# Last four experts: gate and up loaded as whole matrices, the final weights' spread moved behind the transposes, and part of the way back moved ahead of the last product

## The chip, the cores and the metric

The kernel runs on one core of one Trainium2 chip. The metric is the device time of one execution in microseconds, lower is better. The executions of the kernel before took 438.43 to 440.27 us, with a median of 439.71 us.

## What is computed

One decoder layer on 256 tokens of width 1024, in fp32. Two attention mixers and a cross-attention come first. Then comes a mixture of experts: 32 experts in 4 groups, every token goes to its best group and there to its two best experts. A final RMS norm with a gain closes the layer. The part that matters here:

```
hid = (silu(einsum('nd,edf->nef', hf, w_gate[g]))
       * einsum('nd,edf->nef', hf, w_up[g]) * combine[:, g, :, None])
out = out + einsum('nef,efd->nd', hid, w_down[g])
...
x = x + hier_moe(rmsnorm(x, ffn_norm_g[l]), ...)
return rmsnorm(x, final_norm_g)
```

Each expert has a gate and an up matrix of 1024 x 256 and a down matrix of 256 x 1024, all of them 1 MB. The weights of all 32 experts, 96 MB, are read once from the chip's main memory; this stream lasts through the second half of the kernel.

## The kernel before

**Quads and slots.** The experts are worked through four at a time, a "quad". For one quad 32 tokens per expert are gathered, so that the four experts fill the 128 columns of the array side by side, each in a tile of 32. A quad's weights are 12 chunks of 1 MB (MOE_CHUNKS): chunks 0 to 7 are gate and up, chunks 8 to 11 are down. They land in 24 slots of 8 KB per partition; two neighbouring slots make one tensor `moe_pair`. SyncE (SP) issues all loads in one fixed order. It waits for `chunk_used` before each, a count that TensorE raises when it has read a chunk. All weights travel in one queue, first in first out, and some 20 to 28 us of them are queued ahead of what is being moved.

**One quad on TensorE** goes like this: gather(0) for the first half of k, the 1024-long contraction being cut into 8 steps of 128 (gather, L1760, writes the banks `score0` and `score1`; VectorE multiplies by gains and copies to `moe_x`, L1317); the gate and up products of k 0 to 3; gather(1) into the same banks and the same `moe_x`; the gate and up products of k 4 to 7. ScalarE makes silu of the gate product (L887) and VectorE multiplies by the up product (L1335, `hid`). TensorE transposes the selection matrix (L1844) and then `hid` (L1848), and ScalarE copies the latter out (L889, `hidT`). Then follow the down products and the "way back": a product with the weighted selection `selwT` that adds the experts' results to the tokens' sums in the banks ACC (`attno0`, `attno1` for the first 512 columns of tokens 0 to 127 and 128 to 255, `proj1`, `probt1` for the second 512).

**Formats of the loads.** Quad 0's first use is loaded in small runs. Quads in the middle are "whole" (`load_whole`): one DMA for each matrix of one expert, with 8 KB in a row on each partition. The last quad (experts 28 to 31, `load_last`, L456 to L469) is loaded for an early start of its products: gate and up as (half of k, gate or up, pair of experts), two DMAs of 512 KB for each chunk, with 4 KB runs (`load_gate_or_up`, L436); down as columns of all four experts, 2 KB runs, and the last chunk in two parts with 1 KB runs (L468).

**The last quad** (`last_quad`) differs in three ways from the others. Its gate and up products go by (half of k, gate or up) as the chunks come (`gate_up_by_columns`, L1814): gate k 0 to 3, up k 0 to 3, gather(1), gate k 4 to 7, up k 4 to 7. Ahead of that last piece it spreads the row of final gains to all 128 partitions by two products with a row of ones (L1803, into `score0` and `score1`); VectorE copies them to `fin_g` (L1332). And its second 512 columns come in two pieces of 256 (`down_last_columns`, L1894), which VectorE copies to `y1_last` (L1348), and then the way back in four products (`back_last_columns`, L1900). ScalarE squares the finished sums for the final norm (L655); means, root and scaling follow (L921, L594, L1373, L1375, L911), and the output goes out in four DMAs.

An fp32 product appears in the trace as two MATMUL records: a row "x32" is 16 products.

## Time and profile before

| | us |
|---|---|
| median of the timed executions | 439.71 |
| lowest and highest of them | 438.43, 440.27 |
| the profiled execution, whole | 438.02 |
| its span (first to last instruction) | 436.3 |
| TensorE busy | 395.9 (91%) |
| VectorE / ScalarE / GpSimd busy | 190.4 / 155.0 / 36.0 |

The span is what the trace shows; the 1.7 us between it and 438.02 lie around it. Of the 436.3 us about the last 30 belong to the last quad. The shares of busy time are averages over unlike stages, so they say little about a change in the last 30 us; for that one reads the chain of waits and the order in time in this stretch.

### The profile page before, as it was taken

What the parts mean: (1) busy time and instruction counts of PE and PEld (TensorE: products, weight loads), DVE (VectorE), ACT (ScalarE), POOL (GpSimd) and SP (SyncE); (2) the same over time, 40 slices, a digit from 0 to 9 for tenths busy, and PEclk for the clock granted to TensorE, in tenths of its full rate; (3) what the DMA queues carried; (4) which work ended last, traced back from release to release, by engine and by line L of the source; (5) the groups of instructions that cost most, each with busy time, mean ns of one, the idle gap of its engine ahead of it and who ended that gap; (6) DMA issues with size and microseconds to landing.
All of it is one profiled execution on the core that took longest, in us unless ns stands there. A gap on an engine that the chain in (4) does not pass through costs nothing.

```text
span 436.3 us, 7016 instructions
## 1 busy us (share of the span) xinstructions
PE 395.9 (91%) x2761; PEld 278.0 (64%) x2761; DVE 190.4 (44%) x358; ACT 155.0 (36%) x299; POOL 36.0 (8%) x80
## 2 busy tenths in 40 slices
PE   7999999999999999999999989899878838758984
PEld 7998897777788888999796634434333303313632
DVE  3675667866667846754655211221212102102123
ACT  6633565576358444485737110100000000001013
POOL 4010122224000000010401200000000000000001
PEclk9999999999999999999999999999999959969999
DMA  7978776767777668897758899999999999999993
GB/s 243 302 223 281 231 263 215 235 206 241 258 241 268 202 232 292 276 332 225 270 218 361 331 424 421 415 420 421 422 422 423 421 421 422 421 421 409 409 380 120
DMA packets 48770, 138.95 MB, mean 318 GB/s; under 512 B 5191, under 2 KB 19559, under 8 KB 39528
## 3 DMA queue, kind: packets, MB, share of 16 engines
q1 hardware_dynamic: 48528, 138.31, 85.0%
q8 instruction: 17, 0.28, 0.3%
q10 hardware_dynamic: 216, 0.28, 0.2%
q14 instruction: 9, 0.07, 0.0%
HBM read 137.54 MB, written 1.05 MB: 318 GB/s over the span
## 4 chain that ended last, share of the span: by engine, by line
PE 75%; DMA 12%; SPq 5%; DVE 3%; ACT 1%; issue 1%; POOL 1%; DVEq 0%; POOLq 0%; ACTq 0%
DMA moe_pair<-in_expert_w_up_dram 12%; PE proj L1407 10%; PE proj L1408 9%; PE proj L1409 9%; PE proj L1833 7%; SPq L428 5%; PE score L1760 4%; PE score L1856 4%; PE attno L1408 2%; PE attno L1409 2%; PE attno L1407 2%; PE attno L1905 2%; PE proj L1787 2%; PE attno L1551 1%; PE probt L1409 1%; PE probt L1408 1%
## 5 line engine op out<-in xcount | busy, mean ns | idle before, releaser
L945 DVE TENSOR_TENSOR w_lo<-w_raw,w_hi 128x1024 fp32r<-128x1024 f32 x64 | 78.3, 1226 | 37.1 <-ACT w_hi L682 36.8
L682 ACT ACTIVATE w_hi<-w_raw 128x1024 fp32r<-128x1024 f32 x64 | 67.9, 1060 | 40.4 <-DMA w_raw<-in_w_in_dram 11.1
L1833 PE MATMUL proj<-moe_pair,moe_x 128*32 128x512 f32 x384 | 47.4, 637 | 19.6 <-DMA moe_pair<-in_expert_w_up_dram 19.6
L1317 DVE TENSOR_TENSOR moe_x<-score,gains_moe 128x256 f32<-128x256 f32 x32 | 13.6, 425 | 93.3 <-PE score L1760 93.1
L887 ACT ACTIVATE hid<-proj 128x256 f32<-128x256 f32 x8 | 3.1, 383 | 136.8 <-PE proj L1833 112.8
L1833 PEld LDWEIGHTS proj<-moe_pair,moe_x 128*32 128x32 f32 x384 | 11.8, 116 | 45.9 <-issue 44.8
L1760 PEld LDWEIGHTS score<-sel,xg 128*128 128x128 f32 x256 | 30.5, 192 | 10.6 <-issue 10.0
L1407 PE MATMUL proj<-hT_hi,w_hi 128*128 128x256 f32 x112 | 32.3, 288 | 0.8 <-DVE w_lo L1024 0.8
L1760 PE MATMUL score<-sel,xg 128*128 128x128 f32 x256 | 32.5, 279 | 0.0
L1409 PE MATMUL proj<-hT_hi,w_lo 128*128 128x256 f32 x112 | 31.7, 283 | 0.0
L1408 PE MATMUL proj<-hT_lo,w_hi 128*128 128x256 f32 x112 | 31.7, 283 | 0.0
L1856 PE MATMUL score<-moe_pair,hidT 128*32 128x512 f32 x240 | 27.4, 595 | 3.8 <-ACT hidT L889 3.8
L594 POOL TENSOR_TENSOR rnorm<-mean_eps,mhalf 128x1 f32<-128x1 f32 x10 | 5.8, 586 | 299.2 <-DVE mean_eps L921 299.2
L1407 PE MATMUL proj<-w_hi,hT_hi 128*128 128x512 f32 x64 | 25.9, 404 | 0.0
L1408 PE MATMUL proj<-w_lo,hT_hi 128*128 128x512 f32 x64 | 25.0, 391 | 0.0
L1409 PE MATMUL proj<-w_hi,hT_lo 128*128 128x512 f32 x64 | 25.0, 391 | 0.0
L610 POOL TENSOR_SCALAR scores<-scores,rinv 128x128 f32<-128x128 f32 (+1 forms) x32 | 18.1, 584 | 64.7 <-DVE rinv L983 64.7
L1407 PEld LDWEIGHTS proj<-hT_hi,w_hi 128*128 128x128 f32 x112 | 21.4, 191 | 2.2 <-DVE w_lo L1024 1.0
L1408 PEld LDWEIGHTS proj<-hT_lo,w_hi 128*128 128x128 f32 x112 | 21.4, 191 | 0.0
L1409 PEld LDWEIGHTS proj<-hT_hi,w_lo 128*128 128x128 f32 x112 | 21.4, 191 | 0.0
L708 ACT ACTIVATE scores<-scores,nmax 128x128 f32<-128x128 f32 (+1 forms) x32 | 14.2, 445 | 14.7 <-DVE sink_arg L970 7.7
L1856 PEld LDWEIGHTS score<-moe_pair,hidT 128*32 128x32 f32 x240 | 7.0, 109 | 18.5 <-issue 12.8
(345 smaller groups left out, 731.9 us busy)
## 6 DMA issues: line engine op xcount, KB each, us to landing
moe_pair<-in_expert_w_gate_dram SPq DMA_DIRECT2D x28, 1024.0 KB, 13.2
moe_pair<-in_expert_w_up_dram SPq DMA_DIRECT2D x28, 1024.0 KB, 15.0
moe_pair<-in_expert_w_down_dram SPq DMA_DIRECT2D x27, 1024.0 KB, 24.9
w_raw<-in_w_in_dram SPq DMA_DIRECT2D x33, 512.0 KB, 4.4
moe_pair<-in_expert_w_down_dram SPq DMA_DIRECT2D x10, 512.0 KB, 6.5
w_raw<-in_xattn_wkv_dram SPq DMA_DIRECT2D x8, 512.0 KB, 4.4
w_raw<-in_mix_out_w_dram SPq DMA_DIRECT2D x8, 512.0 KB, 5.0
moe_pair<-in_expert_w_gate_dram SPq DMA_DIRECT2D x8, 512.0 KB, 20.1
```

The costliest lines, as they stand in the source:

```text
L428: sp.dma_start(slots[s][:].unsqueeze(1), src).then_inc(moe_in[s], 16)
L610: pool.tensor_scalar(scores[:, j % 2, hh, cols], scores[:, j % 2, hh, cols], rinv[:, j % 2, i:i + 1], 1.0, ALU.mult, ALU.mult).then_inc(s_ ...
L682: act.activation(w_hi[g % NS][:], w_raw[:, g % NW], ACT.Copy).then_inc(hi_done, 1)
L708: act.activation(scores[:, b, hh, cols], scores[:, b, hh, cols], ACT.Exp, bias=nmax[:, b, tt, hh:hh + 1], accum_out=rsum[:, b, i:i + 1]).t ...
L945: dve.tensor_tensor(w_lo[g % NS][:], w_raw[:, g % NW], w_hi[g % NS][:].bitcast(F32), ALU.subtract)\
L1317: dve.tensor_tensor(moe_x[:, pair], SC[u % 2][:, 0:2 * P].rearrange("p (k s) -> p k s", k=2), gains_moe[:, u // 2, pair].unsqueeze(2) .bro ...
L1407: pe.matmul(ps, a[0], b[0], start=start, stop=False, skip_group_check=True)
L1408: pe.matmul(ps, a[0], b[1], start=False, stop=False, skip_group_check=True)
L1409: return pe.matmul(ps, a[1], b[0], start=False, stop=stop, skip_group_check=True)
L1760: op = pe.matmul(SC[u % 2][:, (k % 2) * P:(k % 2 + 1) * P], xg[:, t, k * P:(k + 1) * P], sel[:, t].rearrange("p e s -> p (e s)"), start=t ...
L1833: op = pe.matmul(PJ[0][e * WIN:(e + 1) * WIN, :].rearrange("p (j f) -> p j f", j=2), moe_x[:, k % 4, e * WIN:(e + 1) * WIN], pair[:].rearr ...
L1856: return pe.matmul(SC[half][e * WIN:(e + 1) * WIN, :], hidT[:, kt, e * WIN:(e + 1) * WIN], weights, start=kt == 0, stop=kt == KF - 1)
```

## The change

1. Gate and up of the last quad are loaded as whole matrices of one expert, 8 DMAs of 1 MB with 8 KB runs in place of 16 of 512 KB with 4 KB runs: first the four gates, then the four ups. The down loads stay as they were.
2. TensorE does all of gate (k 0 to 3, gather(1), k 4 to 7), then all of up; it waits for all four gates ahead of the one and for all four ups ahead of the other. As up k 0 to 3 now comes after the second gather, the gathered tokens of the second half get a buffer of their own, `moe_x_late`. ScalarE's silu waits for the gate alone.
3. The spread of the final gains is cut in two: its first product stands between the transposes of `hid` and the first down product (bank `proj0`), its second between the two steps of the first down product (bank `score1`). VectorE copies both after `hid` and `selwT`.
4. The way back of the last 512 columns is no longer one block at the end: the first product for tokens 0 to 127 stands before the last down product, the one for tokens 128 to 255 right after it. The semaphore is raised by each product, and the squares wait for two.

```diff
             def load_last(c):
                 s, e0 = slot_of_chunk(LAST_QUAD * MOE_CHUNKS + c), NE - QE
                 if c < GU_CHUNKS:
-                    load_gate_or_up(c, s, e0, ends_in[c])
+                    j, e = divmod(c, QE)
+                    sp.dma_start(slots[s][:].unsqueeze(1), whole_v[j][:, e0 + e:e0 + e + 1, :])\
+                        .then_inc(ends_in[c], 16)
...
-            expert_quad(more * 2 + 3, GU_CHUNKS - 2)
+            expert_quad(more * 2 + 3, QE)
...
-                    act.wait_ge(back_ps[t][half], more * 2 + 4)
+                    act.wait_ge(back_ps[t][half], more * 2 + 4 + half)
...
-                    dve.tensor_tensor(moe_x[:, pair],
+                    gathered = moe_x_late if next_experts is None and u >= 2 else moe_x
+                    dve.tensor_tensor(gathered[:, pair],
...
-                if next_experts is None:
-                    for h in range(2):
-                        dve.wait_ge(fin_g_ps, h + 1)
-                        dve.tensor_copy(fin_g[:, h * 512:(h + 1) * 512], SC[h][:]).then_inc(fin_g_set, 1)
                 dve.wait_ge(silu_done, n + 1)
...
                 if next_experts is None:
+                    for h, bank in enumerate((PJ[0], SC[1])):
+                        dve.wait_ge(fin_g_ps, h + 1)
+                        dve.tensor_copy(fin_g[:, h * 512:(h + 1) * 512], bank[:]).then_inc(fin_g_set, 1)
                     dve.wait_ge(fin_g_set, 2)
...
+            def gate_then_up(n):
+
+                for j in range(2):
+                    for e in range(QE):
+                        pe.wait_ge(ends_in[j * QE + e], LAST_WHOLE_LANDED)
+                    for k in range(KD):
+                        if j == 0:
+                            if k == KD // 2:
+                                gather(1)
                             if k % 2 == 0:
                                 pe.wait_ge(moe_x_sb, n * 4 + k // 2 + 1)
+                        gathered = (moe_x, moe_x_late)[k // 4]
+                        for e in range(QE):
+                            w = slots[slot_of_chunk(LAST_QUAD * MOE_CHUNKS + j * QE + e)][:]
+                            op = pe.matmul((PJ[0][:, 0:FE], LAST_UP)[j][e * WIN:(e + 1) * WIN],
...
             def back_last_columns(t, i):
 
-                return pe.matmul(ACC[t][1][:, i * CW:(i + 1) * CW], selwT[:, t * P:(t + 1) * P],
-                                 y1_last[:, i * CW:(i + 1) * CW], start=False, stop=True, skip_group_check=True)
+                pe.wait_ge(y1_sb_set, i + 1)
+                pe.matmul(ACC[t][1][:, i * CW:(i + 1) * CW], selwT[:, t * P:(t + 1) * P],
+                          y1_last[:, i * CW:(i + 1) * CW], start=False, stop=True, skip_group_check=True)\
+                    .then_inc(back_ps[t][1], 1)
...
             def last_quad(n):
 
-                gate_up_by_columns(LAST_QUAD, n, ends_in, LAST_UP)
+                gate_then_up(n)
+                transposes(n, hid_halves)
+                pe.wait_ge(fin_in, 16)
+                pe.wait_ge(ones_row_set, 1)
+                spread_gains(PJ[0], 0)
+                pe.wait_ge(hidT_sb, n + 1)
+                down_first_columns(0)
+                pe.wait_ge(selT_sb, n + 1)
+                spread_gains(SC[1], 1)
+                down_first_columns(1).then_inc(y0_ps, 1)
                 pe.wait_ge(fin_g_set, 2)
-                transposes(n, hid_halves)
-                pe.wait_ge(hidT_sb, n + 1)
-                down_first_columns().then_inc(y0_ps, 1)
-                pe.wait_ge(selT_sb, n + 1)
                 pe.wait_ge(y_act, n + 1)
                 back_to_tokens(0, 0)
                 back_to_tokens(1, 0)
...
                 down_last_columns(0, 1).then_inc(y1_ps, 1)
+                back_last_columns(0, 0)
                 pe.wait_ge(last_cols_in, 16)
                 down_last_columns(1, 1).then_inc(y1_ps, 1)
+                back_last_columns(1, 0)
                 for t in range(TT):
-                    for i in range(2):
-                        pe.wait_ge(y1_sb_set, i + 1)
-                        op = back_last_columns(t, i)
-                    op.then_inc(back_ps[t][1], 1)
+                    back_last_columns(t, 1)
```

The order on TensorE, first around the up product of the last quad and the spread. `proj0` holds the gate product, `probt0` the up product; names that begin with `first_and_last_loaded` are the landings of the last quad's chunks. Before:

```order
L1814 MATMUL proj0<-moe_pair8_93,moe_x_107 32x256 [waits moe_x_sb]
L1814 MATMUL proj0<-moe_pair8_93,moe_x_107 32x256 x7
L1803 MATMUL score0<-g_row_125,ones_row_126 128x512 [waits ones_row_set,fin_in]
L1803 MATMUL score1<-g_row_125,ones_row_126 128x512
L1814 MATMUL probt0<-moe_pair9_94,moe_x_107 32x256 [waits moe_x_sb,first_and_last_loaded7,first_and_last_loaded6]
L1814 MATMUL probt0<-moe_pair9_94,moe_x_107 32x256 x7
L1814 MATMUL probt0<-moe_pair9_94,moe_x_107 32x256 [waits moe_x_sb]
L1814 MATMUL probt0<-moe_pair9_94,moe_x_107 32x256 x7
```

The same place after the change:

```order
L1799 MATMUL proj0<-moe_pair6_91,moe_x_late_126 32x256 x2
L1799 MATMUL proj0<-moe_pair7_92,moe_x_late_126 32x256 x2
L1799 MATMUL probt0<-moe_pair8_93,moe_x_107 32x256 [waits first_and_last_loaded6,first_and_last_loaded7,first_and_last_loaded5,first_and_last_loaded4]
L1799 MATMUL probt0<-moe_pair8_93,moe_x_107 32x256
L1799 MATMUL probt0<-moe_pair9_94,moe_x_107 32x256 x2
L1799 MATMUL probt0<-moe_pair8_93,moe_x_107 32x256 x2
```

The spread is gone from here, and the wait for the last two chunks, which stood ahead of 16 products of up, now stands with that for two more ahead of all 32.

From the transposes of `hid` to the first way back, before:

```order
L1848 MATMUL probt0<-ident_152,hid_110 128x128 [waits hid_done]
L1848 MATMUL probt0<-ident_152,hid_110 128x128
L1856 MATMUL score0<-moe_pair10_95,hidT_111 32x512 [waits first_and_last_loaded8,hidT_sb]
L1856 MATMUL score0<-moe_pair10_95,hidT_111 32x512 x3
L1856 MATMUL score0<-moe_pair10_95,hidT_111 32x512 [waits first_and_last_loaded9]
L1856 MATMUL score0<-moe_pair10_95,hidT_111 32x512 x3
L1905 MATMUL attno0<-y0_sb_108,selwT_112 128x512 [waits y_act,selT_sb]
```

and after:

```order
L1833 MATMUL probt0<-ident_153,hid_110 128x128 [waits hid_done]
L1833 MATMUL probt0<-ident_153,hid_110 128x128
L1875 MATMUL proj0<-g_row_125,ones_row_127 128x512 [waits ones_row_set,fin_in]
L1841 MATMUL score0<-moe_pair10_95,hidT_111 32x512 [waits first_and_last_loaded8,hidT_sb]
L1841 MATMUL score0<-moe_pair10_95,hidT_111 32x512 x3
L1875 MATMUL score1<-g_row_125,ones_row_127 128x512 [waits selT_sb]
L1841 MATMUL score0<-moe_pair10_95,hidT_111 32x512 [waits first_and_last_loaded9]
L1841 MATMUL score0<-moe_pair10_95,hidT_111 32x512 x3
L1896 MATMUL attno0<-y0_sb_108,selwT_112 128x512 [waits y_act,fin_g_set]
```

One spread product now stands ahead of each step of the first down product.

The end of TensorE's program, before:

```order
L1894 MATMUL score1<-moe_pair11_96,hidT_111 32x256 [waits first_and_last_loaded11]
L1894 MATMUL score1<-moe_pair11_96,hidT_111 32x256 x3
L1894 MATMUL probt0<-moe_pair11_96,hidT_111 32x256 [waits last_columns_loaded]
L1894 MATMUL probt0<-moe_pair11_96,hidT_111 32x256 x3
L1900 MATMUL proj1<-y1_last_124,selwT_112 128x256 [waits y1_sb_set] x2
L1900 MATMUL probt1<-y1_last_124,selwT_112 128x256 [waits y1_sb_set] x2
```

and after:

```order
L1883 MATMUL score1<-moe_pair11_96,hidT_111 32x256 [waits first_and_last_loaded11]
L1883 MATMUL score1<-moe_pair11_96,hidT_111 32x256 x3
L1890 MATMUL proj1<-y1_last_124,selwT_112 128x256 [waits y1_sb_set]
L1883 MATMUL probt0<-moe_pair11_96,hidT_111 32x256 [waits last_columns_loaded]
L1883 MATMUL probt0<-moe_pair11_96,hidT_111 32x256 x3
L1890 MATMUL probt1<-y1_last_124,selwT_112 128x256 [waits y1_sb_set]
L1890 MATMUL proj1<-y1_last_124,selwT_112 128x256 [waits y1_sb_set]
L1890 MATMUL probt1<-y1_last_124,selwT_112 128x256 [waits y1_sb_set]
```

The last down product now stands behind a wait for VectorE's copy of the one before it.

## Rows read from the trace of the kernel before

**Rows 1.** The page: the span, and the span in 40 slices of 10.9 us.

```profile
span 436.3 us, 7016 instructions
...
DMA  7978776767777668897758899999999999999993
```

**Rows 2.** DMA view: packets and rate from 381 to 393 us, whole matrices.

```profile
DMA packets 695, 5.05 MB, mean 421 GB/s; under 512 B 78, under 2 KB 78, under 8 KB 78
```

**Rows 3.** DMA view: the same from 397 to 413 us, last quad's gate and up.

```profile
DMA packets 1798, 6.55 MB, mean 410 GB/s; under 512 B 198, under 2 KB 198, under 8 KB 1798
```

**Rows 4.** One load each: issue (start us, us) and us to landing. Chunk 7, chunk 9, last columns.

```profile
400.70 0.43 SPq L436 DMA_DIRECT2D moe_pair<-in_expert_w_up_dram  x1
moe_pair<-in_expert_w_up_dram SPq DMA_DIRECT2D x1, 512.0 KB, 15.9
...
404.27 4.38 SPq L468 DMA_DIRECT2D moe_pair<-in_expert_w_down_dram  x1
moe_pair<-in_expert_w_down_dram SPq DMA_DIRECT2D x1, 1024.0 KB, 17.8
...
415.88 2.54 SPq L468 DMA_DIRECT2D moe_pair<-in_expert_w_down_dram  x1
moe_pair<-in_expert_w_down_dram SPq DMA_DIRECT2D x1, 512.0 KB, 11.6
```

**Rows 5.** The chain that ended last, in time: start us, us, what.

```profile
408.95 1.86 PE proj L1814 x32
...
412.54 1.98 PE score L1760 x16
414.53 1.86 PE proj L1814 x32
416.39 1.91 PE score L1803 x4
418.30 1.94 PE probt L1814 x32
...
420.73 0.45 PE probt L1848 x2
...
421.64 1.97 PE score L1856 x16
...
424.38 1.95 PE attno L1905 x4
...
427.33 0.48 PE score L1894 x8
...
427.83 0.44 DVE y_last L1348
...
428.31 1.14 PE proj L1900 x4
429.45 0.88 PE probt L1900 x4
```

**Rows 6.** Timeline, ScalarE's squares at the end and TensorE's down product for the last columns.

```profile
427.58 0.63 PE L1894 MATMUL probt<-moe_pair,hidT 128*32 128x256 f32 x8
...
429.49 0.60 ACT L655 ACTIVATE fin_rows<-proj 128x512 f32<-128x512 f32 x1 [2.44 <-PE proj L1900]
429.99 0.20 ACT L655 ACTIVATION_READ_ACCUMULATOR fin_rows<-proj 128x1 f32 x1
...
430.36 0.60 ACT L655 ACTIVATE fin_rows<-probt 128x512 f32<-128x512 f32 x1 [0.17 <-PE probt L1900]
```

**Rows 7.** Stretches: us, busy PE, PEld, DVE, ACT, POOL, granted clock, DMA share, GB/s.

```profile
324.40:326.70 2.30, 0.00 (x0) 0.00 (x0) 0.41 (x1) 0.00 (x0) 0.00 (x0) 1.00 1.01 420
326.80:330.40 3.60, 3.60 (x33) 1.00 (x33) 0.00 (x0) 0.00 (x0) 0.00 (x0) 1.00 1.02 423
386.50:392.10 5.60, 5.60 (x33) 1.22 (x33) 0.00 (x0) 0.00 (x0) 0.00 (x0) 0.63 1.01 421
```

More of the change, by code:

```diff
@@ L1790, in gate_up_first @@
                     op.then_inc(chunk_used, 1)
-            def gate_up_by_columns(q, n, arrived, up):
-                for kh in range(KH):
-                    if kh == 1:
-                        gather(1)
-                    for j in range(2):
-                        if q == LAST_QUAD and kh and j:
-                            pe.wait_ge(fin_in, 16)
-                            pe.wait_ge(ones_row_set, 1)
-                            for h in range(2):
-                                pe.matmul(SC[h][:], ones_row[:], g_row[:, h * 512:(h + 1) * 512], start=True, stop=True)\
-                                    .then_inc(fin_g_ps, 1)
-                        for pair in range(2):
-                            pe.wait_ge(arrived[kh * QE + 2 * j + pair], LAST_LANDED)
-                        for r in range(RUN):
-                            k = kh * RUN + r
+            def gate_then_up(n):
[6 more added lines that the diff above has]
+                                gather(1)
@@ new lines, in gate_then_up @@
+                        for e in range(QE):
+                            w = slots[slot_of_chunk(LAST_QUAD * MOE_CHUNKS + j * QE + e)][:]
+                            op = pe.matmul((PJ[0][:, 0:FE], LAST_UP)[j][e * WIN:(e + 1) * WIN],
+                                           gathered[:, k % 4, e * WIN:(e + 1) * WIN],
+                                           w.rearrange("p (k f) -> p k f", k=KD)[:, k], start=k == 0,
+                                           stop=k == KD - 1, skip_group_check=True)
+                            if k == KD - 1:
+                                op.then_inc(chunk_used, 1)
@@ L1877, in down_whole, with down_first_columns, spread_gains @@
                 return op
-            def down_first_columns():
-                for kt in range(KF):
-                    c = GU_CHUNKS + kt
-                    pe.wait_ge(ends_in[c], LAST_LANDED)
-                    w = slots[slot_of_chunk(LAST_QUAD * MOE_CHUNKS + c)]
-                    for e in range(QE):
-                        op = down_product(0, kt, e, w[:, e * 512:(e + 1) * 512])
-                return op
+            def down_first_columns(kt):
+                c = GU_CHUNKS + kt
+                pe.wait_ge(ends_in[c], LAST_LANDED)
+                w = slots[slot_of_chunk(LAST_QUAD * MOE_CHUNKS + c)]
+                for e in range(QE):
+                    op = down_product(0, kt, e, w[:, e * 512:(e + 1) * 512])
+                return op
+            def spread_gains(bank, half):
+                pe.matmul(bank[:], ones_row[:], g_row[:, half * 512:(half + 1) * 512], start=True, stop=True)\
+                    .then_inc(fin_g_ps, 1)
             def down_last_columns(i, kt):
```

20 lines of the change are left out of this document (2 added, 18 removed).

## The prediction

> **What bounds the kernel now.** I read the page's slices first. In the second half the DMA engines are busy without a break until just before the end [rows 1]: the expert weights arrive back to back, and everything up to the last quad is paced by them. The change leaves that part alone, so I take it as fixed up to 408.95 us, where the last quad's first product starts [rows 5]. What is left is the question what paces the last 27 us, TensorE or the stream. For that I read the landings of single loads beside the chain that ended last.
>
> Chunk 7, the last of up, lands at 400.70 + 15.9 = 416.6 us [rows 4]. TensorE starts the product that needs it at 418.30, behind the spread of the gains (416.39, 1.91 us) [rows 5]. Chunk 9 lands at 404.27 + 17.8 = 422.1, and TensorE reaches it half way through the down product that starts at 421.64, at about 422.6 [rows 4, 5]. The last columns land at 415.88 + 11.6 = 427.5, and the product on them starts at 427.58 [rows 4, 6]. So TensorE sets the pace in this stretch, and the stream catches up with it only at the very end, where the two are 0.1 us apart. The chain agrees: from 408.95 to 430.33 it is all TensorE, with the short hand-overs that each quad has. Work taken from TensorE here counts in full; work added counts in full too, unless it stands in one of its waits.
>
> **Part 1, the loads.** Whole matrices travel at 421 GB/s [rows 2], the 4 KB runs of the last quad at 410 [rows 3]. Gate and up are 8.39 MB: 20.46 us at 410, 19.93 at 421. The stretch begins at 416.6 - 20.46 = 396.1. So the four gates are there at 396.1 + 9.96 = 406.1, well before TensorE asks for them, and the four ups at 416.1, 0.5 us earlier than now. SP issues 8 DMAs in place of 16; with 12 to 18 us between issue and landing [rows 4] that has no price, and nothing else queued on SP is waited for.
> By the Trainium skill (DMA: Bandwidth & Descriptors, Specifications) transfers run at line rate from 512 B up. By that rule 4 KB and 8 KB runs would be equal and the ups would still land at 416.6; the two rates above say otherwise, and I go by them.
>
> **Part 2, gate, then up.** Gate k 0 to 3 takes 1.86 us, the gather 1.98, gate k 4 to 7 another 1.86 [rows 5]: TensorE is through at 408.95 + 5.70 = 414.65. VectorE's copies of the gathered tokens come one gather pair (1 us) ahead of their use, as now. Then up needs all four matrices: TensorE waits until 416.1, 1.45 us. All 32 products of up come after that, two times 1.86, to 419.85. Before, up ended at 418.30 + 1.94 = 420.24. So although 1.91 us of spread have left, the gain is only **0.4 us**: before, only 16 products stood behind the last landing, now 32 do. Bounds: if the ups land at 416.6 there is a loss of 0.1. Nothing can be gained beyond 0.4, unless the ups come sooner than 421 GB/s lets them. Silu, 1.5 us earlier, was not waited for before either.
>
> A 1.45 us wait is new, and the clock could answer it. The profile shows half the clock only after long stops: after 7.76 us of idle, 16 products of L1833 take 5.60 us at a mean clock of 0.63, while a stop of 2.4 us before 326.76 leaves the clock at 1.00 and the same work takes 3.60 [rows 7]. I take no loss, since 1.45 is below the stop that did no harm. At half the clock all of up would take 3.7 us more; that is a rival.
>
> **Part 3, the spread.** Two products take 1.91 us, 0.95 each; the first two of the way back, which are as wide, take 1.95, and four half as wide 1.14 + 0.88 [rows 5]. The first now stands where TensorE waits for ScalarE's copy of hidT: its transposes end at 420.73 + 0.45 = 421.18 and the down product starts at 421.64, so 0.46 of it is hidden and it costs **0.5 us** (0.4 if it runs at 0.88, the pace of two half-width products in the last row). The second stands between the two steps of the down product. Is there a wait that hides it? Chunk 9 will land at about 422.1 - 0.5 = 421.6. In the new order TensorE has the hid transposes done at 420.8, the first spread at 421.75 and the first down step at 422.7, so chunk 9 has been there for 1.1 us and nothing is hidden: **+0.95 us**. That is the second term of importance. Bounds: 0 (if the chunk landed after 423.6, 2 us late) to 0.95. VectorE's two copies of the gains move behind `hid` and `selwT`; the second can start at 423.65 and is twice as wide as the copy that took 0.44 [rows 5], so it ends by 424.6, before the way back asks for it at 425.4, and costs nothing. The sum so far is -0.4 + 0.5 + 0.95 = +1.05: the down product ends 1.05 later than 423.61, and all up to the end of the third last-columns product (427.81) moves along, since ScalarE's and VectorE's steps there hang on TensorE.
>
> **Part 4, the end.** Call T the end of the third product (427.33 + 0.48 = 427.81 before). Before, the fourth ran while VectorE copied the first half of y1 (427.83, 0.44), and the way back started at T + 0.50 and ended at 430.33, T + 2.52 [rows 5]. Now the first way-back product stands between them and waits for that copy with TensorE idle: it runs from T + 0.50 to T + 1.05 (1.14 for two), the fourth product until T + 1.5, VectorE's second copy until T + 1.95, the product for tokens 128 to 255 under it. Then the two products of the second half: T + 2.0 to T + 2.5 and T + 2.95. That is 0.45 later than before. ScalarE squares `proj1` from T + 2.5 (before 429.49 = T + 1.68, because both products on `proj1` came first) and is free for the next 0.70 later (0.50 to the read of the sum, 0.20 for that) [rows 6]: `probt1` from T + 3.25, before 430.36 = T + 2.55. The means, the root and the output follow the second square as before. So the order costs **+0.7 us** in all, from 0.45 (if the squares come closer together) to 0.75. The wait for the last columns is now later, at T + 1.05 with T at 428.86, and the landing at 427.0; it falls away, but it was only 0.1 us.
>
> **Sum.** -0.4 + 0.5 + 0.95 + 0.7 = +1.75 us, from +1.2 (small ends of parts 3 and 4) to +2.3 (no faster landing). Against the profiled execution 438.02 + 1.75 = 439.8. The median of the timed executions is 1.7 us above the profiled one; the same step on it is 439.71 + 1.7 = **441.4**. What can be told from no change in this kernel is about 0.5%, or 2.2 us; the step is 0.4%.
>
> **Rivals.**
> *The stream holds TensorE in the last quad* (no change at all). In the profiled execution stream and TensorE meet at 427.5. The timed executions are up to 2.2 us longer, and the trace does not show where. If in them the down chunks land late, the second spread and the way back do stand inside waits, as the last products then wait for the landing in both kernels. From a landing 1.7 us later than profiled the two are level. Difference -0.5 (the faster gate and up) to +0.5, 439.2 to 440.2. For it: the two are close at the end. Against: the weights ahead of the last quad come by the same stream and move its start along.
> *Slower: the landing of the ups without the gain in rate*. By the rule cited above the ups land at 416.6: +2.3 us, 442.0, just over the limit of 2.2.
> *Slower: the new stop drops the clock*. It decides from the point at which a stop of 1.45 us, between 2.4 us that did nothing and 7.76 that did, is enough. Up at half clock: +3.7, but after the 7.76 us stop the clock was back after some products, and the loss was 5.60 - 3.60 = 2.0 us [rows 7]. So +2.0 to +3.7 on top of 1.75: 443.5 to 445.2.
> *Faster*. Between the rows of the chain from 408.95 to 430.33 TensorE stands idle for at most 0.49 us (420.24 to 420.73), 0.46 (to 421.64), 0.77 (423.61 to 424.38) and 0.1 (to 428.31), 1.8 in all [rows 5]. If all of it were filled, the gain would still be below 2.2. Only late landings of over 4 us could give more.
> *It does not do what it says*: the spread was to go inside waits. By part 3 and 4 only 0.46 us of it does; that is in the forecast.
>
> **How the numbers follow.** Forecast (+1.2 to +2.3) 0.62; stream holds TensorE 0.17; no gain in rate 0.09; clock 0.06; faster by a mechanism that I do not see 0.06. The range takes the forecast on either end of the scatter of medians (about 0.7 us) and reaches down into the first rival: 439.0 to 442.8. The forecast lies 0.45 us under the limit of 0.5%, so a quarter of it falls beyond: slower 0.16 + 0.05 + 0.06 = 0.27. Faster 0.06. Same 0.67.
>
> **What would show it.** In the profile after: the four ups' last issue to landing gives about 416.1; TensorE idle some 1.4 us before the first product on `probt0`, waiting for a DMA; up done at 419.8 (part 2). The first product of the spread takes 0.95 and the down product starts 0.5 after hidT is ready, and the step on chunk 9 starts right after the second spread, waiting for no DMA (part 3). TensorE idle for about 0.45 before the first product on `proj1`, and the last square at about 432.1 in place of 430.36 (part 4). I am wrong if chunk 9 or the last columns are still waited for, if the clock falls below 1.00 after 416, or if the whole quads before 408.95 move.

## The result

The changed kernel takes 442.78 us, the median of 20 executions (440.27 to 445.91). The kernel before takes 439.18 beside it (20 executions, 438.43 to 440.27). The ratio is 1.0084 with a 95% interval of 1.0068 to 1.0100: **slower by 3.6 us or 0.8%**, where I forecast 441.4 and a step of 1.7. The step is about twice the one I worked out. That the time lies in the range (439.0 to 442.8) by 0.02 us is luck: the range was set on a median of 439.71 for the kernel before, 0.5 us above the 439.18 measured. The changed kernel also scatters more: 5.6 us from its fastest to its slowest execution, against 1.8. One execution each of e3, e6 and e18 below took 466, 2218 and 799 us, far from all others, and is left out of their medians and counts.

The profiled execution took 442.26 us. From its page come the span, the granted clock and the DMA share in 40 slices (as [rows 1]):

```profile
span 440.5 us, 7009 instructions
...
PEclk9999999999999999999999999999999969869998
DMA  7978776767777667897668999999999999999982
```

The DMA engines are busy to the end here too. From the DMA view of 399 to 414 us, the last quad's gate and up as whole matrices (as [rows 3]):

```profile
DMA packets 873, 6.35 MB, mean 423 GB/s; under 512 B 98, under 2 KB 98, under 8 KB 99
```

The chain that ended last, in time: start us, us, what (as [rows 5]; the first piece is chunk 7's load, from issue to landing, as [rows 4]):

```profile
389.70 27.86 DMA moe_pair<-in_expert_w_up_dram
417.56 0.14 issue
417.69 3.75 PE probt L1799 x64
...
421.95 0.44 PE probt L1833 x2
422.39 1.05 PE proj L1875 x2
423.44 1.00 PE score L1841 x8
424.44 1.05 PE score L1875 x2
425.49 1.04 PE score L1841 x8
...
427.29 1.96 PE attno L1896 x4
...
430.25 0.48 PE score L1883 x8
...
430.75 0.43 DVE y_last L1341
...
431.22 0.70 PE proj L1890 x2
431.92 0.57 PE probt L1883 x8
432.49 0.63 PE probt L1890 x2
433.12 0.63 PE proj L1890 x2
...
433.77 0.70 ACT fin_rows L648 x2
...
434.79 0.58 POOL rnorm L587
```

The chain has the shape that I drew: one stop for a load before up, then TensorE without a wait for a load, and the new order at the end.

**A fair pair.** The span is 4.2 us longer than that of [rows 1], more than the medians differ. The first product on an expert shows why. The three rows are from TensorE's timelines: the recorded profile of before, the changed kernel, and a second profile of before (run e6_before_again, below), in this order:

```profile
241.50 0.86 PE L1787 MATMUL proj<-moe_pair,moe_x 128*32 128x256 f32 x12 [0.71 <-DVE moe_x L1317]
```

```profile
243.21 1.07 PE L1780 MATMUL proj<-moe_pair,moe_x 128*32 128x256 f32 x16 [0.71 <-DVE moe_x L1311]
```

```profile
243.10 0.64 PE L1787 MATMUL proj<-moe_pair,moe_x 128*32 128x256 f32 x8 [0.71 <-DVE moe_x L1317]
```

Up to there the code is the same in all three. The recorded profile of before is 1.6 us ahead of the second one for no reason in the code. The second profile and that of the changed kernel start level, so I compare these two. Its page and its chain:

```profile
span 438.3 us, 7016 instructions
```

```profile
420.38 1.93 PE probt L1814 x32
...
423.72 1.97 PE score L1856 x16
...
429.41 0.48 PE score L1894 x8
...
430.39 1.13 PE proj L1900 x4
431.52 0.88 PE probt L1900 x4
...
432.42 0.70 ACT fin_rows L655 x2
```

Before against changed: up ends at 420.38 + 1.93 = 422.31 and at 421.44 (**-0.87**). From there to the start of the down product it is 1.41 and 2.00 (**+0.59**), the down product takes 1.97 and 3.09 (**+1.12**), from its end to T (the end of the third last-columns product) it is 4.20 in both, and from T to the end of the span 8.4 and 9.8 (**+1.4**). The sum is +2.2 us. It depends a little on the traces: from the first product on an expert to the end of the span the two traces of before take 194.8 and 195.2 us, and the two of the changed kernel (this one and e5's) 197.3 each. So the change costs 2.1 to 2.6 us in a trace in which the clock is full throughout the last quad; 3.3 to 3.6 was measured in the medians. Two things have to be explained: terms that were mis-sized, and 0.7 to 1.5 us that these traces don't show at all.

### The profile page after: what moved, and what is told of

The parts are those of the page before. It is cut to its first block, busy times and chain, and to the rows that moved or that the text cites. A ratio compares the mean times of both kernels' runs of the same rounds, so it can differ in the third digit from the quotient of the medians.

```text
span 440.5 us, 7009 instructions
## 1 busy us (share of the span) xinstructions
PE 401.0 (91%) x2761; PEld 279.7 (63%) x2761; DVE 190.5 (43%) x358; ACT 154.9 (35%) x299; POOL 36.0 (8%) x80
## 3 DMA queue, kind: packets, MB, share of 16 engines
HBM read 137.54 MB, written 1.05 MB: 315 GB/s over the span
## 4 chain that ended last, share of the span: by engine, by line
PE 71%; DMA 14%; SPq 6%; DVE 4%; ACT 2%; issue 1%; POOL 1%; DVEq 0%; POOLq 0%; ACTq 0%
DMA moe_pair<-in_expert_w_up_dram 13%; PE proj L1400 9%; PE proj L1401 9%; PE proj L1402 9%; PE proj L1818 7%; PE score L1841 4%; PE score L1753 4%; SPq L427 3%; SPq L452 3%; PE attno L1896 2%; PE proj L1780 2%; DMA w_raw<-in_mix_out_w_dram 2%; PE attno L1400 2%; PE attno L1544 1%; PE attno L1402 1%; PE attno L1401 1%
## 5 line engine op out<-in xcount | busy, mean ns | idle before, releaser
L1818 PE MATMUL proj<-moe_pair,moe_x 128*32 128x512 f32 x384 | 50.0, 668 | 17.2 <-DMA moe_pair<-in_expert_w_up_dram 17.2
L1311 DVE TENSOR_TENSOR moe_x<-score,gains_moe 128x256 f32<-128x256 f32 x30 | 12.7, 425 | 88.8 <-PE score L1753 88.7
```

What stands on the lines that cost most here:

```text
L1818: op = pe.matmul(PJ[0][e * WIN:(e + 1) * WIN, :].rearrange("p (j f) -> p j f", j=2), moe_x[:, k % 4, e * WIN:(e + 1) * WIN], pair[:].rearr ...
```

## The experiments

Medians are us, beside the kernel before on the same chip; the runs e1 to e4 were on one chip, e5 and e8 to e10 on a second, e6, e11, e13 and e16 on a third, e17 to e20 on a fourth. The last column counts executions whose mean granted clock over the whole span was 0.966 or less; why this matters comes with e2.

| run | median | before | ratio (95%) | low clock |
|---|---|---|---|---|
| e1_loads_order | 439.47 | 438.94 | 1.0007 (0.9989 to 1.0026) | 0 of 12 |
| e2_spread_only | 440.86 | 438.94 | 1.0036 (1.0012 to 1.0061) | 6 of 12 |
| e3_end_only | 440.00 | 438.94 | 1.0029 (1.0014 to 1.0044) | 0 of 11 |
| e4_after_old_end | 440.65 | 438.94 | 1.0042 (1.0023 to 1.0061) | 2 of 12 |
| e5_after_again | 442.32 | 439.02 | 1.0082 (1.0064 to 1.0101) | 0 of 6 |
| e6_before_again | 438.58 | 438.97 | 0.9994 (0.9983 to 1.0006) | 0 of 11 |
| e8_fill_stop | 443.45 | 439.02 | 1.0076 (1.0049 to 1.0102) | 2 of 6 |
| e9_full_spread | 442.70 | 439.02 | 1.0075 (1.0054 to 1.0095) | 0 of 6 |
| e10_spread_only_full | 439.01 | 439.02 | 1.0001 (0.9987 to 1.0015) | 0 of 12 |
| e11_fill_and_full | 441.09 | 438.97 | 1.0054 (1.0039 to 1.0069) | 0 of 6 |
| e13_second_in_y0_wait | 441.21 | 438.97 | 1.0050 (1.0030 to 1.0070) | 0 of 6 |
| e16_end_no_wait | 439.58 | 438.97 | 1.0013 (1.0001 to 1.0024) | 0 of 12 |
| e17_padded_y0 | 439.08 | 439.01 | 1.0002 (0.9992 to 1.0013) | 0 of 11 |
| e18_onerow_y0 | 439.10 | 439.01 | 1.0005 (0.9990 to 1.0020) | 2 of 11 |
| e19_spread_only_padded | 438.45 | 439.01 | 0.9989 (0.9980 to 0.9998) | 0 of 13 |
| e20_after_padded | 441.73 | 439.01 | 1.0072 (1.0057 to 1.0087) | 0 of 6 |

The ratio is not the quotient of the two medians. In runs of six executions the two part by up to 1.1 us: e8 is +4.4 by the medians and +3.3 by the ratio, e9 +3.7 and +3.3, e20 +2.7 and +3.2, e11 +2.1 and +2.4. Differences of that size between these runs are not to be read.

### Which part costs how much: e1 to e4, and repeats e5, e6

**e1_loads_order** is before with parts 1 and 2 alone: the loads as in the change, the spread in the stop ahead of up, the old end.

```diff
...
 for j in range(2):
+    if j:
+        pe.wait_ge(fin_in, 16)
+        pe.wait_ge(ones_row_set, 1)
+        for h in range(2):
+            spread_gains(SC[h], h)
     for e in range(QE):
         pe.wait_ge(ends_in[j * QE + e], LAST_WHOLE_LANDED)
...
```

> Parts 1 and 2 alone: whole loads, gate then up, but both products of the spread stand between gate and up, in the stop before the ups' landing, and the end is the old one. Theory A (the step is the sum of local terms of the last quad): the spread (1.9 us) fills the stop of about 1.1 to 1.5 us and pushes up by 0.4 us at most, so within 0.5 us of the kernel before, and as little scatter as there (1.9 us from lowest to highest). Theory B (the whole loads or the later up product bring the scatter, since the changed kernel scatters over 5.6 us and its median lies 0.8 us above what its profile explains): 1 to 2 us slower, scatter of 4 us or more.

The median is +0.5, not to be told from nothing; Theory B's 1 to 2 us didn't come, though the executions scatter over 3.7 us. So the faster loads bring no time that could be measured, though they land as forecast. Its trace shows why its profiled execution didn't gain: the clock. Chain, then the stretches (us, busy PE, PEld, DVE, ACT, POOL, granted clock, DMA share, GB/s):

```profile
418.29 5.44 PE probt L1805 x64
```

```profile
417.00:418.20 1.20, 1.07 (x3) 0.18 (x1) 0.78 (x2) 0.00 (x0) 0.00 (x0) 1.00 1.01 374
418.30:423.70 5.40, 5.40 (x65) 3.38 (x66) 0.50 (x1) 0.00 (x0) 0.00 (x0) 0.68 1.05 386
```

Up takes 5.44 us here and 3.75 in the changed kernel, at a mean clock of 0.68. Ahead of it stand only the spread's products and a stop of 0.22 us for a load, much less than the 1.45 us stop that I had weighed. So the stop's length alone cannot be what decides.

**e2_spread_only** is part 3 alone: `spread_gains` behind the transposes and between the down steps, everything else as before.

```diff
...
-pe.wait_ge(fin_g_set, 2)
 transposes(n, hid_halves)
+pe.wait_ge(fin_in, 16)
+pe.wait_ge(ones_row_set, 1)
+spread_gains(PJ[0], 0)
 pe.wait_ge(hidT_sb, n + 1)
-down_first_columns().then_inc(y0_ps, 1)
+down_first_columns(0)
 pe.wait_ge(selT_sb, n + 1)
+spread_gains(SC[1], 1)
+down_first_columns(1).then_inc(y0_ps, 1)
+pe.wait_ge(fin_g_set, 2)
```

> Part 3 alone: the spread behind the transposes and inside the down product, old loads, old order, old end. Theory A: up starts 1.6 us earlier at its landing, the two products add 0.6 and 1.05 us later, and the second now overlaps the landing of chunk 9: 0 to +0.3 us against the kernel before. Theory B: the same here; a scatter above 3 us would speak for the spread as its source.

It missed: +1.9. The single executions say how. Six ran at a mean clock of 0.965 and took 440.85 to 442.61 us; six ran at 0.973 to 0.979 and took 437.79 to 440.88. No execution of before in this study was under 0.968. A mean lower by 0.011 (0.965 against 0.976, the mean of the other six) over 440 us is by estimate some 10 us more at half the clock (0.011 x 440 / 0.5). e2's own trace is one of the six others (0.978), so where in the program these 10 us lie is not seen. Other traces bound it. In that of e10, with a mean of 0.969, the clock is at 0.50 in three stretches of the whole quads, of 3.4, 10.2 and 10.2 us (the rows show the last two), and in the last 3.3 us, in which TensorE has nothing to do:

```profile
352.20:362.40 10.20, 4.78 (x24) 1.20 (x28) 0.00 (x0) 0.00 (x0) 0.00 (x0) 0.50 1.01 419
383.00:393.10 10.10, 5.68 (x28) 1.40 (x32) 0.00 (x0) 0.00 (x0) 0.00 (x0) 0.50 1.01 421
```

No kept trace has more of it than that outside the last quad, but for up to 1.1 us more after TensorE's last product (e16, mean 0.968). So an execution at 0.965 has by estimate some 3 us of half the clock beyond them. The count misses falls too: the traces of e1 and e8, which do show one in the last quad, have means of 0.969 and 0.968. With that said, moving two small products, without any new stop for a load, brought executions at a mean clock that no version with them ahead of up had: 6 of 12 here, none of 101 of before, none in e1, e3, e6 and e16. That these are falls to half the clock (from 2.4 to 1.2 GHz) in the last quad is argued, not seen.

**e3_end_only** is part 4 alone.

```diff
...
 down_last_columns(0, 1).then_inc(y1_ps, 1)
+back_last_columns(0, 0)
 pe.wait_ge(last_cols_in, 16)
 down_last_columns(1, 1).then_inc(y1_ps, 1)
+back_last_columns(1, 0)
 for t in range(TT):
-    for i in range(2):
-        pe.wait_ge(y1_sb_set, i + 1)
-        op = back_last_columns(t, i)
-    op.then_inc(back_ps[t][1], 1)
+    back_last_columns(t, 1)
```

> Part 4 alone: the first way-back products ahead of and right behind the last down product, all else old. Theory A: +1.3 to +1.4 us (in the trace of the changed kernel the output leaves 5.27 us after the third last-columns product, before 3.90). My prediction had +0.7. Scatter as before. If the old kernel really waits for the last columns in its timed executions, less than +1.0.

+1.1 us. Its chain, from the first product of the way back:

```profile
428.41 0.70 PE proj L1901 x2
429.11 0.57 PE probt L1894 x8
429.68 0.63 PE probt L1901 x2
430.31 0.63 PE proj L1901 x2
...
430.96 0.70 ACT fin_rows L655 x2
```

The same durations as in the changed kernel, and none of the 0.43 to 0.5 that I had used. From T to the end of the span it is 9.8 us in this trace, 1.4 more than before, as expected; the median shows 1.1.

**e4_after_old_end** is the changed kernel with the old end, the diff of e3 backwards.

> The changed kernel with part 4 undone. Theory A: 1.3 to 1.4 us faster than the changed kernel, so +2.2 us against the kernel before (ratio 1.005), with the scatter of 4 us or more kept if it comes from parts 1 to 3.

+1.7, where Theory A had +2.2. With e3's +1.1 that is 2.8: both halves of the change cost, and the sum still lies under the 3.3 to 3.6 of the whole.

**e5_after_again** and **e6_before_again** are the changed kernel and the kernel before, with no edit.

> The changed kernel once more, for a second trace and to see its scatter beside the next three. All theories: +3.0 to +4.0 us against the kernel before. Theory C (the clock falls inside the last quad in part of the executions): the executions above 443 us have a mean clock of 0.970 or less, those below 442 us of 0.972 or more.

> The kernel before once more, for a second trace. Its profiled execution (438.02 us) was faster than every timed one (438.43 to 440.27), and in the seven traces of other variants the matmuls ahead of the experts, which no variant touches, start 0.8 to 2.2 us later than in that trace. If that trace was a lucky one: a span of 437 to 438 us here, the first expert product 0.8 us or more later than 241.5 us, and from the landing of the last whole quad to the end 40.1 us as before.

The step repeats on another chip: +3.3 us, 1.0082. The clocks are as Theory C had them, on one execution each: 443.95 us at 0.969, 441.76 at 0.973. e6 gives the fair pair above; its first expert product comes 1.6 us later than in the recorded profile, as expected, its span of 438.3 us is just above the 437 to 438.

### The order of the end: e16

Before's end, with the way back ordered by halves but all of it behind the last down product. It tells what the order by halves costs ScalarE's first square apart from what the wait and the alternation cost.

```diff
...
 down_last_columns(1, 1).then_inc(y1_ps, 1)
-for t in range(TT):
-    for i in range(2):
-        pe.wait_ge(y1_sb_set, i + 1)
-        op = back_last_columns(t, i)
-    op.then_inc(back_ps[t][1], 1)
+for i in range(2):
+    for t in range(TT):
+        back_last_columns(t, i)
```

> The kernel before with the way back of the last columns ordered by halves (first half for both token tiles, then second half) but all of it behind the last down product, so that TensorE never waits for a copy with nothing to do. It splits the +1.36 us of part 4 (seen in the traces): if the lateness comes from the first square, whose sum is now complete after three products and not two, +0.3 to +0.5 us here and 0.9 from the wait; if all comes from the wait for the copy and the changes between narrow and wide products, 0.

+0.6 by the medians; its trace has 0.4 more from T to the end than before, as forecast. Its chain:

```profile
429.80 0.70 PE proj L1901 x2
430.50 0.43 PE probt L1901 x2
430.93 0.45 PE proj L1901 x2
...
431.40 0.70 ACT fin_rows L655 x2
```

The products cost 0.43 and 0.45 when no 32-column down product stands between them, against 0.63 in e3. So of the 1.4 us that part 4 costs in the traces, 0.4 is the later first square (both halves of `proj1` must be there first), and about 0.9 is the down product that now stands between the products of the way back and the dearer switches around it. The wait and the switches are not told apart.

### Is it the stop or the one-row products: e8, e9, e11

All three are the changed kernel. **e8_fill_stop** puts one product of 128 rows, which nothing uses, into the stop ahead of up. **e9_full_spread** gives the spread's products 128 rows (its gains are then wrong). **e11_fill_and_full** does both.

```diff
...
 for j in range(2):
+    if j:
+        for _ in range(1):
+            pe.matmul(SC[0][:], ident[:], xg[:, 0, 0:512], start=True, stop=True)
```

```diff
-pe.matmul(bank[:], ones_row[:], g_row[:, half * 512:(half + 1) * 512], start=True, stop=True)\
+pe.matmul(bank[:], ident[:], xg[:, 0, half * 512:(half + 1) * 512], start=True, stop=True)\
```

> The changed kernel with one more full-width product (128 rows, 0.95 us, its result unused) between gate and up, inside the stop before the ups' landing, which was 1.06 us in the trace. Theory A (only local terms): no change to the changed kernel, or +0.1 us where the landing comes early. Theory C1 (the stop ahead of up lets the clock fall): 0.5 to 1.5 us faster than the changed kernel in the median, and scatter down from 5.6 to under 3 us. Theory C2 (the products of the spread, with one row of the array in use, let it fall): no change.

> The changed kernel with both products of the spread using 128 rows of the array (identity by gathered tokens) and not one; equal width and duration. The final gains are wrong by that. Theory A: no change to the changed kernel. Theory C1: no change. Theory C2: 0.5 to 1.5 us faster in the median, and no executions with a mean clock under 0.970.

> The changed kernel with both: one more 128-row product in the stop ahead of up, and 128 rows in both products of the spread (final gains wrong by that). Theory C (the clock falls in the last quad because of the stop or of the one-row products): 441.0 to 441.8, no execution above 442.5. Theory A: 442.3 to 442.8 as the changed kernel.

The filled stop alone brings nothing (+4.4, with an interval that overlaps that of the changed kernel), and the scatter of 4.7 us stays: Theory C1 missed. Its trace is the clearest of the study. Chain, then the stretches around:

```profile
424.73 1.25 PE score L1878 x2
425.99 1.91 PE score L1844 x8
...
428.66 3.75 PE attno L1899 x4
```

```profile
417.00:425.40 8.40, 7.18 (x80) 3.52 (x80) 1.45 (x3) 0.38 (x1) 0.00 (x0) 1.00 1.06 382
425.50:432.30 6.80, 5.99 (x13) 1.38 (x12) 1.38 (x2) 1.29 (x3) 0.00 (x0) 0.50 0.25 82
```

The clock falls during the second one-row product (L1878), which takes 1.25 in place of 1.05, and stays at 0.50 for 6.8 us. The down step takes 1.91 in place of 1.04 and the way back 3.75 in place of 1.96. It falls in work, not in a stop: up to there TensorE was busy 7.18 of 8.40 us, and in the stretch itself 5.99 of 6.80. The Trainium skill (TensorE: Matmul & The Clock Gate, Part 1) ties the clock to how busy TensorE has been recently; the busy share of these rows doesn't show such a want. From the end of up to 425.4 us TensorE was busy 3.52 of 3.75 us here and 3.72 of 3.95 in the changed kernel's own trace, in which the clock stayed at 1.00.

With 128 rows alone (e9) the step is +3.7 and no execution is under 0.969. Theory C2 had it 0.5 to 1.5 us faster than the changed kernel, and it is not: it missed too. Both together (e11) give +2.1, the first result that is the sum of the local terms (its trace takes 197.4 us from the first expert product to the end, as the changed kernel's), with 1.3 us between the fastest and the slowest of six executions. Over 416.5 to 433 us its trace has the full clock:

```profile
416.50:433.00 16.50, 14.71 (x132) 6.45 (x132) 4.37 (x8) 2.93 (x8) 0.00 (x0) 1.00 0.57 202
```

### Part 3 with 128 rows: e10, e19, e20

**e10_spread_only_full** is e2 with e9's edit (gains wrong). **e19_spread_only_padded** is e2 computed rightly: `g_row` gets 127 rows of zeros.

```diff
-g_row = sb("g_row", [1, D], F32, slot_at[4])
-ones_row = sb("ones_row", [1, P], F32, slot_at[5])
+g_row = sb("g_row", [P, D], F32, slot_at[4])
+ones_row = sb("ones_row", [P, P], F32, slot_at[5])
...
-act.dma_start(g_row[:], final_norm_g.rearrange("(a n) -> a n", a=1)).then_inc(fin_in, 16)
+act.wait_ge(ones_row_set, 1)
+act.dma_start(g_row[0:1, :], final_norm_g.rearrange("(a n) -> a n", a=1)).then_inc(fin_in, 16)
...
+dve.memset(g_row[:], 0.0).then_inc(ones_row_set, 1)
...
-pe.wait_ge(ones_row_set, 1)
+pe.wait_ge(ones_row_set, 2)
```

> Part 3 alone as in e2_spread_only, with 128 rows in both products of the spread (final gains wrong by that). e2 had six of twelve executions at a mean clock of 0.965 and 440.9 to 442.6 us, against 437.8 to 440.9 for the others. Theory C2: the six vanish, median 439.0 to 439.8. Theory C1 (a stop ahead of up of 0.56 us in e2's trace) and theory A: as e2, 440.9.

> Part 3 alone as in e2_spread_only, computed rightly over 128 rows: the row of gains padded with 127 rows of zeros, a 128 x 128 block of ones as weights, zeros and ones set by VectorE after the last whole quad. If what matters is the rows of the array that are in use, as in e10_spread_only_full (128 rows of tokens, no loss against the kernel before): within 0.4 us of the kernel before and no execution at a mean clock of 0.965. If what matters is that data other than zero go through: as e2_spread_only, +1.9 us, and part of the executions at 0.965.

e10 takes 439.01, level with before, and e19 438.45, if anything a little faster (0.9989, well within the 0.5% that I called no difference). e2 with one row took 440.86. The place in the program, the number of products and their columns are the same; only the rows differ, and what fills them. No execution of e10 or e19 was at 0.965, against 6 of 12 of e2. The first product is also a little shorter with 128 rows (the second, between the down steps, is not: 1.06 and 1.05); chains of e10 and e2:

```profile
420.85 0.86 PE proj L1882 x2
```

```profile
421.32 1.05 PE proj L1882 x2
```

**e20_after_padded** is the changed kernel with e19's edit.

> The changed kernel with the padded 128-row spread, the stop ahead of up unfilled. Local terms alone give +2.2 us against the kernel before. If the one-row products carry the rest of the changed kernel's loss: +2.0 to +2.6. If the stop ahead of up carries it: +3 or more, as the changed kernel and e9_full_spread.

+2.7, between e11 (+2.1) and the changed kernel (+3.3 to +3.6); the intervals overlap on both sides. By the ratio it is +3.2, level with e9.

Over all runs: with one-row products behind the transposes (the changed kernel, e2, e4, e5, e8, e13, e18) 13 of 73 executions were at 0.966 or less; with 128-row products there (e9, e10, e11, e17, e19, e20) none of 54. e2 ran on another chip than e10 and e19, but it isn't the chip: on e2's own, e1, e3 and before had none, and among the runs of one chip it was 2 of 11 (e18) against 0 of 24 (e17, e19), and 2 of 6 (e8) against 0 of 18 (e9, e10). The weak spot is the changed kernel itself. It gives only 1 of the 13 (e5 none of 6), six are e2's, so for it this count says little.

### Another place for the second product: e13, e17, e18

**e13_second_in_y0_wait** is the changed kernel with the second product behind the second down step, where TensorE waits 0.8 us for `y_sb`.

```diff
...
-spread_gains(SC[1], 1)
 down_first_columns(1).then_inc(y0_ps, 1)
-pe.wait_ge(fin_g_set, 2)
+spread_gains(SC[1], 1)
 pe.wait_ge(y_act, n + 1)
...
 back_to_tokens(1, 0)
+pe.wait_ge(fin_g_set, 2)
```

**e17_padded_y0** is the same edit on e19, and **e18_onerow_y0** is e17 with one-row products.

> The changed kernel with the second product of the spread moved from between the two steps of the first down product to behind them, where TensorE waits 0.77 us for ScalarE's copy of y0. Theory A (the second product was exposed in full, 1.05 us plus 0.06 of a slower start after it): 0.7 to 0.9 us faster than the changed kernel. If it had stood in the wait for chunk 9's landing, as the change says: 0.3 us slower than the changed kernel at the most, no gain.

> As e19, and the second product of the spread in TensorE's wait for the copy of y0. If rows count: TensorE is about 1 us earlier at the last columns and then waits for their landing, so 0.4 to 0.9 us faster than the kernel before (ratio 0.998 to 0.999), which 0.5% can not tell. If data count: 0 to +1.5 us.

> As e17 with the one-row products of the changed kernel. If one-row products let the clock fall: 1 to 2 us slower than e17 in the median and a scatter above 3.5 us. If the clock in e2 had another cause: as e17.

e13 takes 441.21, 1.1 to 1.6 less than the changed kernel; in the traces, from the first expert product to the end, it is 0.9 less (196.4 against 197.3). So the second product had stood in no wait, and the new place was a better one. e17 takes 439.08: the 0.4 to 0.9 us that were expected didn't show in the median, which is no better than e19's. Its timeline shows what is late next:

```profile
423.20 1.07 PE L1850 MATMUL score<-moe_pair,hidT 128*32 128x512 f32 x8 [0.63 <-DMA moe_pair<-in_expert_w_down_dram]
...
428.66 0.64 PE L1892 MATMUL probt<-moe_pair,hidT 128*32 128x256 f32 x8 [0.18 <-DMA moe_pair<-in_expert_w_down_dram]
```

TensorE, now earlier, waits for chunk 9 and then for the last columns: the stream holds the end of this version, so time taken from TensorE ahead of these landings is lost again in the wait for them. e18 (1.0005) has the same median, so the 1 to 2 us expected of one-row products didn't come; but its 11 executions scatter over 4.2 us, and two were at 0.965, at 441.08 and 442.53 us. So the one-row products seem to keep their risk at this place too, in fewer executions.

## Why the prediction was right and wrong

**What bounds the kernel: right.** In the last quad of the changed kernel TensorE waits once for a load, as said. Neither chunk 9 nor the last columns are waited for. e17 confirms how close the stream is.

**Part 1, the loads: right.** The rate was 423 GB/s (used: 421) [rows 2, 3]. Chunk 7 lands at 417.56; in e6, whose stream is level with it, it does so at 418.1, so the gain is 0.5 to 0.6 (forecast: 0.5). The Trainium skill (DMA: Bandwidth & Descriptors, Specifications) has transfers at line rate from 512 B up. These traces don't agree: 8 KB runs moved at 421 and 423 GB/s, 4 KB runs at 410, and the 2 KB runs of the down loads, in DMAs of 1 MB like the first, at 387 (the row of the changed kernel under "The clock").

**Part 2, gate then up: right in form.** The stop before up is in the timeline:

```profile
417.69 1.93 PE L1799 MATMUL probt<-moe_pair,moe_x 128*32 128x256 f32 x32 [1.06 <-DMA moe_pair<-in_expert_w_up_dram]
```

It is 1.06 us long (forecast: 1.45). Up ends 0.87 earlier than in e6, whose TensorE reached it late, and relative to the stream 0.3 earlier than in the recorded profile (421.44 - 420.24 = 1.2, less the 1.5 by which the stream is late); the forecast was 0.4. e1 says that nothing of this reaches the median.

**Part 3, the spread: a little short.** +0.59 for +0.5 and +1.12 for +0.95, since a product takes 1.05 and not 0.95. My row, 1.91 for two products back to back, averaged over a pair; alone between products of another kind each takes 1.05. At the first place 128 rows take 0.86 (e10), so there it is the one row; at the second 128 rows take 1.06, so there it is the neighbours.

**Part 4, the end: a step that failed; the term was half its size.** "The order costs +0.7 us in all" measured +1.4 (pair of traces) and +1.1 (e3, medians). I priced each switch between down product and way back at the 0.43 to 0.5 that they take among their own kind. They take 0.57 to 0.70. So ScalarE's first square starts at 433.77 = T + 3.04, where I had T + 2.5. What I had wrong besides is the path behind the squares. Timeline, ScalarE's squares:

```profile
433.77 0.60 ACT L648 ACTIVATE fin_rows<-proj 128x512 f32<-128x512 f32 x1 [3.81 <-PE proj L1890]
...
434.36 0.59 ACT L648 ACTIVATE fin_rows<-probt 128x512 f32<-128x512 f32 x1
```

I said that the last square starts 0.7 later and the output follows it. The squares are only 0.59 apart, and the last one, at T + 3.63 (before: T + 2.55), is no longer what the output waits for: the chain goes from the two squares into the root (434.79, 0.58) and to VectorE. Before, the root was not in the chain, but the first square's root ended at 431.08, level with VectorE's mean of the second square at 431.13. So what delays the output is the first square's move, from T + 1.68 to T + 3.04, and that is the 1.4 us. Of it 0.8 was in my own numbers (T + 2.5), had I followed the first square; the rest is the price of the switches.

**The clock: the other step that failed, as far as is known.** "I take no loss, since 1.45 is below the stop that did no harm." With parts 3 and 4 at their measured sizes the sum would have been some +2.7 (traces: +2.1 to +2.6); the medians have 0.7 to 1.5 us more, and I had put them at nothing. The stop alone was too little to look at (filling it in e8 changed nothing), and one profile too little to look in. In the changed kernel's own trace the last quad runs at a clock of 1.00:

```profile
417.69:421.45 3.76, 3.76 (x65) 2.53 (x66) 0.00 (x0) 0.00 (x0) 0.00 (x0) 1.00 1.05 387
```

If the clock costs anything, it does so in other executions. Nine of the 20 had a mean clock of 0.970 or less and a median of 443.84; the other eleven 441.95, 1.9 us less. In the kernel before the same split gives 0.8 us (439.67 for 15 executions, 438.9 for 86), so not all of the 1.9 belongs to the change. e1 and e8 show the fall in the last quad in their traces; no kept trace of the changed kernel itself does. With 128 rows and the stop filled (e11) the step is back at the local terms, +2.1 by the medians and +2.4 by the ratio, though its interval still touches that of the changed kernel. How the rest divides between the one-row products and the stop is not shown: e9 and e20 take away only the one-row products and stay at +3.2 and +3.3 by the ratio, e8 fills only the stop and stays at +3.3. So that the clock causes the rest is argued from the other versions and not shown in this one. A rival stands untested: half the clock in the whole quads, which every trace of before and of the changed kernel shows (after the 2.17 us stop at the end of this document, for one), might cost more here than before. My rival for this (443.5 to 445.2, all of up at half the clock in every execution) had perhaps the right resource, but a trigger that e8 doesn't bear out, and a price that could hold only for a part of the executions.

**The other rivals.** The stream didn't hold TensorE; the gain in rate was there; nothing made it faster. As the rival "It does not do what it says" put it, only about half a us of the spread stands inside a wait.

**What stays open.** Whether the clock carries the rest of the changed kernel's loss, why the rows of a product bear on the clock, and how much of the rest belongs to the stop and how much to the one-row products. No version here beats the kernel before by more than can be told from no change.

## What to carry to other kernels

Price a product by its neighbours: alternating between column-tiled and full-width products took 0.57 to 0.70 us each where a run of one kind took 0.43 to 0.5. Before a tiny product (one row that spreads a vector) moves into a stretch that sets the end, try it padded to 128 rows, and time it in a dozen executions, since a clock that falls in some of them shows in no single profile. And where a load lands only 0.1 us before the engine asks for it, engine time saved ahead of it is lost in the wait for that landing. Before you price the end of a kernel, find which of several instructions the output hangs on, and check that the new order leaves it so.

## What the runs showed of the hardware that I had not expected

The clock can fall while TensorE is busy: in e8 for 6.8 us, 5.99 of them busy, from within a one-row product on. The length of a stop doesn't decide it alone: a stop of 2.4 us in before left the clock at 1.00 [rows 7], while in the changed kernel a stop of 2.17 us, in code that the change doesn't touch, was followed by 32 products in 5.34 us in place of 3.60. TensorE's timeline of the changed kernel:

```profile
328.24 5.34 PE L1818 MATMUL proj<-moe_pair,moe_x 128*32 128x512 f32 x32 [2.17 <-DMA moe_pair<-in_expert_w_up_dram]
```

The work ahead of the experts shifts by 1.6 us from execution to execution, as the first product on an expert shows (241.50 and 243.10 in the same kernel; 241.5 to 244.2 over all versions). A term below that can't be read from two traces without lining them up first.
